# The last output block of a layer kernel in three token parts (256, 128, 128) instead of two of 256

## The reference

```python
x = x + 0.5 * swiglu(rmsnorm(x, ffn2_norm[l]), ffn2_w_gate[l], ffn2_w_up[l], ffn2_w_down[l])
return rmsnorm(x, final_norm)      # x * rsqrt(mean(x*x over the 1024 channels) + EPS) * g
```

## Time and profile before

| | us |
|---|---|
| median of 3 runs (lowest, highest) | 958.43 (958.25, 959.22) |
| the profiled execution's own time | 960.42 |
| its span | 958.6 |
| PE busy | 909.7 (95%), x5672 |
| DVE busy | 702.1 (73%), x1213 |
| ACT busy | 459.2 (48%), x766 |
| POOL busy | 58.2 (6%), x75 |

### The profile page before, as it was taken

One profiled execution on the slowest core, in us unless ns is written; L12 is line 12 of the kernel. 1 busy time (PEld: TensorE's weight loads), 2 busy tenths in 40 slices (PEclk: granted clock), 3 DMA queues, 4 the chain that ended last, 5 costly groups with the idle time before them and its releaser, 6 DMA issues.

```text
span 958.6 us, 15901 instructions
## 1 busy us (share of the span) xinstructions
PE 909.7 (95%) x5672; PEld 819.9 (86%) x5672; DVE 702.1 (73%) x1213; ACT 459.2 (48%) x766; POOL 58.2 (6%) x75
## 2 busy tenths in 40 slices
PE   8769999999999999999989999699999999999995
PEld 5569999999988888888878788599999999888885
DVE  7879999999744343578887676799999998534334
ACT  5455666666523232444772344556666665323220
POOL 4000000000000000000443300000000000000002
PEclk9879999999999999999999999799999999999997
DMA  5123332332343233222211131133323332432312
GB/s 187 61 84 98 106 108 92 109 109 91 107 143 102 97 109 110 75 81 86 67 67 44 66 114 62 44 111 109 109 89 108 109 98 99 132 102 99 107 44 88
DMA packets 40005, 91.73 MB, mean 96 GB/s; under 512 B 4401, under 2 KB 7729, under 8 KB 39969
## 3 DMA queue, kind: packets, MB, share of 16 engines
q1 hardware_dynamic: 39792, 90.79, 29.0%
q0 software_dynamic: 176, 0.46, 0.1%
HBM read 89.14 MB, written 2.10 MB: 95 GB/s over the span
## 4 chain that ended last, share of the span: by engine, by line
PE 42%; DVE 32%; DMA 12%; issue 8%; ACT 5%; DVEq 1%; SPq 0%; ACTq 0%
PE ps L341 14%; PE ps L342 14%; PE ps L343 13%; DMA raw<-weights 11%; DVE w_lo L1256 11%; DVE sums L1248 3%; DVE sums L1237 3%; DVE work L1280 3%; DVE work L1286 1%; DVE work L1288 1%; DVE work L1277 1%; ACT xe_hi L774 1%; DVE sums L1241 1%; ACT w_hi L743 1%; DVE xe_lo L1225 1%
## 5 line engine op out<-in xcount | busy, mean ns | idle before, releaser
L1148 DVE TENSOR_TENSOR w_lo<-raw,w_hi 128x1024 fp32r<-128x1024 f32 x83 | 103.6, 1249 | 127.5 <-ACT w_hi L743 121.3
L426 PE MATMUL ps<-xg_hi,w_hi 128*128 128x256 f32 x640 | 185.5, 290 | 5.1 <-DVE w_lo L1256 3.1
L341 PE MATMUL ps<-act_hi,w_hi 128*128 128x512 f32 (+1 forms) x470 | 180.7, 385 | 3.5 <-DVE act_lo L1154 3.0
L427 PE MATMUL ps<-xg_lo,w_hi 128*128 128x256 f32 x640 | 181.8, 284 | 0.0
L428 PE MATMUL ps<-xg_hi,w_lo 128*128 128x256 f32 x640 | 181.7, 284 | 0.0
L342 PE MATMUL ps<-act_lo,w_hi 128*128 128x512 f32 (+1 forms) x470 | 179.2, 381 | 0.0
L343 PE MATMUL ps<-act_hi,w_lo 128*128 128x512 f32 (+1 forms) x470 | 179.2, 381 | 0.0
L743 ACT ACTIVATE w_hi<-raw 128x1024 fp32r<-128x1024 f32 x75 | 79.2, 1057 | 179.9 <-PE ps L343 172.8
L426 PE MATMUL ps<-xe_hi,w_hi 128*128 128x256 f32 x480 | 136.5, 284 | 17.3 <-ACT work L815 15.7
L428 PE MATMUL ps<-xe_hi,w_lo 128*128 128x256 f32 x480 | 136.0, 283 | 0.0
L427 PE MATMUL ps<-xe_lo,w_hi 128*128 128x256 f32 x480 | 134.8, 281 | 0.0
(11 more groups left out here) (185 smaller groups left out, 1398.1 us busy)
## 6 DMA issues: line engine op xcount, KB each, us to landing
raw<-weights SPq DMA_DIRECT2D x82, 512.0 KB, 3.3
raw<-weights SPq DMA_DIRECT2D x160, 256.0 KB, 2.7
x<-x_t SPq DMA_DIRECT2D x8, 256.0 KB, 4.7
out<-x SPq DMA_DIRECT2D x6, 256.0 KB, 2.2
raw<-weights SPq DMA_DIRECT2D x9, 128.0 KB, 4.4
out<-x SPq DMA_DIRECT2D x4, 128.0 KB, 2.0
raw<-weights SPq DMA_DIRECT2D x1, 384.0 KB, 3.0
arena<-pool_w POOLq DMA_DIRECT2D x1, 256.0 KB, 4.2
```

What stands on the lines that cost most here:

```text
L341: pe.matmul(acc, hi, m_hi, start=first, stop=False)
L426: pe.matmul(acc, hi[:, at], m_hi, start=first and k == 0, stop=False, skip_group_check=True)
L427: pe.matmul(acc, hi[:, at], m_lo, start=False, stop=False, skip_group_check=True)
L1148: dve.tensor_tensor(w_lo[:, k % SLOTS], raw[:, k % RAWS], f32(w_hi[:, k % SLOTS]), ALU.subtract).then_inc(lo_made, 1)
```

## The change

The last block is cut in three parts of 256, 128 and 128 tokens. `LAST` holds for each part its first and last 128-token block and the bank of PSUM it sums in. Part 1 is now tokens 256 to 383, part 2 tokens 384 to 511. Both take 66 passes of 128 tokens. POOL scales parts 0 and 1, DVE part 2. PE does the sums of part 0 before f = 6 of part 1 and those of part 1 before f = 12 of part 2; the spread of part 0 before f = 19 of part 1; and after the last pass the spread of part 1 (into bank 0), the sums of part 2, the spread of part 2. On DVE the first three instructions of part 2 stand behind the inverse square root of part 1, and the copy of part 1's spread value stands between them and part 2's own inverse square root. SP issues 15 stores instead of 10.

```diff
+LAST = ((0, 2, 3), (2, 3, 5), (3, 4, 1))
@@ sync
+            for a, (tb, end, _) in enumerate(LAST):
+                at = slice(tb * P, end * P)
+                made, before = (y_made, 0) if a == 2 else (ya_made, KD * a)
                 for d, n in STORES:
+                    sp.wait_ge(made, before + d + n)
...
@@ tensor, last_blocks
+                def spread_part(a):
                     pe.wait_ge(col_step, STEPS * (4 + a))
+                    dst = ps[:, 6] if a != 1 else ps[:, 0]
+                    spread_columns(dst, range(*LAST[a][0:2])).then_inc(rep_made, 1)
...
-                for a in range(2):
-                    at = slice(a * HALF, (a + 1) * HALF)
+                for a, (tb, end, bank) in enumerate(LAST):
+                    at = slice(tb * P, end * P)
                     for f in range(FB):
...
-                        if a == 1 and f == 6:
-                            mean_of_half(0)
+                        if a >= 1 and f == 6 * a:
+                            mean_of_part(a - 1)
                         if a == 1 and f == 19:
-                            spread_half(0)
+                            spread_part(0)
-                        mm = three_passes(ps[:, 3 + 2 * a, 0:HALF], ...
+                        mm = three_passes(ps[:, bank, 0:(end - tb) * P], ...
                     mm.then_inc(last_made, 1)
-                mean_of_half(1)
-                spread_half(1)
+                spread_part(1)
+                mean_of_part(2)
+                spread_part(2)
@@ gpsimd
+            for a, (tb, end, _) in enumerate(LAST[0:2]):
+                at = slice(tb * P, end * P)
+                pool.wait_ge(last_rinv, a + 1)
+                for d in range(KD):
+                    pool.wait_ge(gained, d + 1 if d < KD - 1 else KD + a)
+                    pool.tensor_tensor(x[:, d, at], x[:, d, at], rinv[:, at], ALU.mult).then_inc(ya_made, 1)
@@ vector, last_block
+                last_of_x(0)
+                inverse_rms(3, slice(*LAST[0][0:2]))
+                keep_rinv(0)
+                last_of_x(1)
+                inverse_rms(4, slice(*LAST[1][0:2]))
+                last_of_x(2)
+                keep_rinv(1)
+                inverse_rms(5, slice(*LAST[2][0:2]))
+                dve.wait_ge(rep_made, 6)
+                at = slice(LAST[2][0] * P, T)
                 for d in range(KD):
-                    dve.wait_ge(gained, d + 1 if d < KD - 1 else KD + 1)
+                    dve.wait_ge(gained, d + 1 if d < KD - 1 else KD + 2)
                     dve.tensor_tensor(x[:, d, at], x[:, d, at], ps[:, 6, at], ALU.mult).then_inc(y_made, 1)
```

More of the change, by code:

```diff
@@ L327, in _ @@
             units(DN2 + RAWS, N_UNITS)
-            for a, made in enumerate((ya_made, y_made)):
-                at = slice(a * HALF, (a + 1) * HALF)
+            for a, (tb, end, _) in enumerate(LAST):
+                at = slice(tb * P, end * P)
+                made, before = (y_made, 0) if a == 2 else (ya_made, KD * a)
                 for d, n in STORES:
-                    sp.wait_ge(made, d + n)
+                    sp.wait_ge(made, before + d + n)
                     sp.dma_start(out[d * P:(d + n) * P, at].rearrange("(n p) t -> p n t", p=P),
                                  x[:, d:d + n, at]).then_inc(stored, 16)
-            sp.wait_ge(stored, 2 * 16 * len(STORES))
+            sp.wait_ge(stored, len(LAST) * 16 * len(STORES))
         @block.tensor
@@ L495, in last_blocks, with mean_of_part @@
             def last_blocks():
-                def mean_of_half(a):
-                    for tb in range(2 * a, 2 * a + 2):
+                def mean_of_part(a):
+                    for tb in range(*LAST[a][0:2]):
                         at = slice(tb * P, (tb + 1) * P)
-                        if a == 0 and tb == 0:
+                        if tb == 0:
                             pe.wait_ge(ssq_made, 4 * KD - 1)
-                        if tb == 2 * a:
+                        if tb == LAST[a][0]:
                             pe.wait_ge(last_sq, a + 1)
@@ L508, in mean_of_half @@
                     mm.then_inc(ms_made, 1)
-                def spread_half(a):
+                def spread_part(a):
                     pe.wait_ge(col_step, STEPS * (4 + a))
-                    spread_columns(ps[:, 6], range(2 * a, 2 * a + 2)).then_inc(rep_made, 1)
+                    dst = ps[:, 6] if a != 1 else ps[:, 0]
+                    spread_columns(dst, range(*LAST[a][0:2])).then_inc(rep_made, 1)
                 for d in range(KD - 4, KD - 1):
@@ L523, in last_blocks @@
                             pe.wait_ge(lo_made, n + 1)
-                        if a == 1 and f == 6:
-                            mean_of_half(0)
+                        if a >= 1 and f == 6 * a:
+                            mean_of_part(a - 1)
                         if a == 1 and f == 19:
-                            spread_half(0)
-                        mm = three_passes(ps[:, 3 + 2 * a, 0:HALF], *weight(n, f % KD), act_hi[:, f, at], act_lo[:, f, at],
+                            spread_part(0)
+                        mm = three_passes(ps[:, bank, 0:(end - tb) * P], *weight(n, f % KD), act_hi[:, f, at], act_lo[:, f, at],
                                           f == 0, f == FB - 1)
                     mm.then_inc(last_made, 1)
-                mean_of_half(1)
-                spread_half(1)
+                spread_part(1)
+                mean_of_part(2)
+                spread_part(2)
             def mixer():
@@ L1640, in last_block, with last_of_x @@
                 d = KD - 1
-                for a in range(2):
-                    at = slice(a * HALF, (a + 1) * HALF)
+                def last_of_x(a):
+                    tb, end, bank = LAST[a]
+                    at = slice(tb * P, end * P)
                     dve.wait_ge(last_made, a + 1)
-                    dve.tensor_tensor(work[:, 0, at], ps[:, 3 + 2 * a, 0:HALF], rinv[:, at], ALU.mult).then_inc(y_scaled, 1)
+                    dve.tensor_tensor(work[:, 0, at], ps[:, bank, 0:(end - tb) * P], rinv[:, at], ALU.mult).then_inc(y_scaled, 1)
                     dve.wait_ge(y_scaled, 2 * KD + a)
@@ L1651, in last_block, with keep_rinv @@
                     dve.tensor_tensor(sq[1][:, at], x[:, d, at], x[:, d, at], ALU.mult).then_inc(last_sq, 1)
-                    inverse_rms(3 + a, slice(2 * a, 2 * a + 2))
+                def keep_rinv(a):
+                    at = slice(LAST[a][0] * P, LAST[a][1] * P)
                     dve.wait_ge(rep_made, 4 + a)
-                    if a == 0:
-                        dve.tensor_copy(rinv[:, at], ps[:, 6, at]).then_inc(last_rinv, 1)
+                    dve.tensor_copy(rinv[:, at], ps[:, 6 * (1 - a), at]).then_inc(last_rinv, 1)
+                last_of_x(0)
[8 more added lines that the diff above has]
+                at = slice(LAST[2][0] * P, T)
                 for d in range(KD):
-                    dve.wait_ge(gained, d + 1 if d < KD - 1 else KD + 1)
+                    dve.wait_ge(gained, d + 1 if d < KD - 1 else KD + 2)
                     dve.tensor_tensor(x[:, d, at], x[:, d, at], ps[:, 6, at], ALU.mult).then_inc(y_made, 1)
```

## The result

The changed kernel takes 974.4 us (median of 4, 973.62 to 975.09), the kernel before 958.69 (4 runs); the ratio is 1.0163, 95% interval [1.0146, 1.0181]. It is 15.7 us slower; the forecast was 962.6, 4.15 us slower, and its range ended at 965.2. The profiled execution has a span of 972.1 us (before 958.6), 13.5 more.

The account below looks back on a forecast made before the run. Bound by when PE's last pass starts plus the serial tail: 7.05 - 1.08 - 1.16 + 0.58 - 0.44 - 1.04 + 0.24 = +4.15 us, carried to the median as 962.6 us; range 959.9 to 965.2.

Parts of the forecast that it names:

- the price of a narrow pass at the full clock: PE's 128-token passes in the last block: 0.110 us each, paced by the weight load, against 0.120 for 256 tokens.
- the stream's term: PE from part 1's first pass: 78 and 70 passes at 0.11 us, last pass at 951.19 instead of 944.14, +7.05 us.
- rival 2: PE's last-block stream: passes of 128 move columns for half as long, so the clock falls; 977 us, chance 3%.
- last pass to the first sum: Tail, three DVE instructions on 128 tokens after the last pass: 2.44 us becomes 1.36, -1.08.
- 12 steps to the spread: Tail, DVE's last inverse root, seven steps slowed to 0.42 us beside POOL: 3.38 us becomes 3.96, +0.58.
- spread: Tail, PE's spread with two passes fewer, at the low clock: 1.32 us becomes 0.88, -0.44.
- eight multiplications: Tail, DVE's final scaling, on 128 tokens instead of 256: 2.73 us becomes 1.69, -1.04.
- last result to the end: Tail, last stores on SP, with results coming faster than SP issues: 2.88 us before, +0.24 after.
- rival 3: DVE's queue: part 1's inverse root ends after part 2's last pass; up to +1.0 us, 963.6, chance 15%.
- rival 4: Tail: POOL holds the last steps longer, 0.737 us each instead of 0.42; +2.4 us, 965.0, chance 10%.
- The four sums: Tail, PE's sums, four passes at the full clock instead of eight: 1.71 us becomes 0.55, -1.16.
- The tail as a whole: Serial work behind PE's last pass, 14.5 us before: DVE, PE sums, inverse root, spread, multiplications and stores, mostly shortened.

Follow-up runs that it names:

- the split alone: Kernel before, with part 1's 66 passes of 256 tokens done as two runs of 66 passes of 128, old tail kept: 974.43 us, ratio 1.0123.

## Why the prediction was wrong

The sign was right, and so was the price of a narrow pass at the full clock: it is not set by its columns, so two parts of 128 cost more than one of 256. The step that failed is the stream's term, +7.05 us, which took the full clock for every pass; the stream measured +17.34. The case that came true is rival 2, "The clock falls in the stream", which was given 3% and a time of 977. The argument against it was: "the sums move one column per pass and the clock stayed full around them". That row doesn't bear on it: in the kernel before the sums stood among passes of 256 columns. Set among passes of 128, they were what brought the clock down, as the run with sums of 128 columns and the run with more sums in the narrow-first order show from both sides. Rival 2 as written was not right either: it laid the fall on the narrow passes alone, which held the full clock for 15.4 us when they came first. Its 977 is near the measured 974.4 because it priced the low clock for all 132 passes, and about 101 ran there. The prediction did name the sign by which it shows: a clock below 1.00 between 936 and 951.

Term by term, with the run with wide sums (full clock) beside the changed kernel:

| us | forecast | changed | sums of 128 columns |
|---|---|---|---|
| part 1's first pass to the last pass | 16.17 | 26.46 | 16.37 |
| last pass to the first sum | 1.36 | 1.51 | 1.38 |
| sums | 0.55 | 1.06 | 0.75 |
| 12 steps to the spread | 3.96 | 3.37 | 3.46 |
| spread | 0.88 | 0.89 | 0.89 |
| eight multiplications | 1.69 | 1.67 | 1.67 |
| last result to the end | 3.12 | 2.93 | 2.89 |
| time | 962.6 | 974.4 | 962.58 |

- The pass of 128 tokens: 0.11 us, right; at the low clock 0.213. About 101 passes of the stream run there (148, less some 47 in the 5.2 us from 934.21 to 939.4), and 101 x 0.102 = 10.3 us is the stream's miss of 10.3. The Trainium skill's 81 ns ("TensorE: Matmul & The Clock Gate", "Back-to-back issue gap") does not hold for these passes: the trace shows 0.111 at the full clock.
- DVE's queue (rival 3) cost nothing: in the run with wide sums DVE had been idle 1.06 us when it began on part 2.
- POOL's eight took 3.35 us as forecast (3.36), not the 5.9 of rival 4. Five steps beside it came 0.35 to 0.42 apart, not seven, so 0.6 us too much was charged. The two with one input (L1184, L1185, on 128x1) took 0.15 each with POOL at work; on 128x2, in the kernel before, the same two (L1178, L1179) took 0.70 and 0.65.
- The four sums were taken at the full clock, 0.55, because PE's wait ahead of them was short. In the changed kernel the clock was already low (1.06). In the run with the sums in two fours, at the full clock, they took 0.64. The reason given is not borne out: after a wait of 2.07 us, in the run where only POOL starts earlier, the sums still met the full clock.
- The tail as a whole: 11.56 forecast, 11.43 measured. What the change set out to shorten got shorter by 3.0 us. It could not pay for the 7.2 us that the stream grew by, even at the full clock: 962.58 against 958.59, ratio 1.0038.

## What to carry to other kernels

In a stream where every matmul has its own weight load, halving the moving columns need not buy time on TensorE: here 0.120 us for 256 columns, 0.112 for 192 and 0.111 for 128. Such a stream can also lose the clock. Look at what else stands in it, products of one column above all, and price the low clock from a run at both levels, not from a row where the same products stood among wide ones. In a serial tail, look first at who shares with the engine that is on it: starting part 0's multiplications earlier took 1.1 us of sharing out of the tail, and moving them from GpSimd to DVE's gap another 0.6, for no work added.

## What was not expected of the hardware

- In the run with the narrow parts first, 15.4 us of passes of 128 columns, 0.111 us apart, held the clock at 2.4 GHz with 4 passes of one column among them. With 8 in a row it went to 1.2 GHz 2.9 to 3.2 us after their first, in the profiled execution of each of the three kernels that had them so. PE was busy without a gap all the while.
- The outcome can differ between executions of one kernel: 961.34 beside 974.25 to 974.92 with the split alone, 975.3 beside 962.81 to 964.28 with the sums in two fours. What decides it in one execution stays open.
- After a fall, narrow passes did not bring the clock back in 21 us (939.4 to 960.67, changed kernel); passes of 256 columns did in 3.3 (943.3 to 946.6, the run with more sums).
- In the tail the clock fell in the eight sums after PE had waited 2.16 us (kernel before), and not after 2.07 us (only POOL earlier).
